# A Fourier layer's loads, spectrum scalings, joins and conditioning rows put in another order

## The chip, the cores and the metric

The kernel runs on one core of one Trainium2 chip. The metric is device time in microseconds (us); the median of three runs of the kernel before is 1674.48 us (1673.05 to 1675.82). The engines are PE (matrix products), DVE (vector), ACT (activations and copies), POOL (a second vector engine) and SP, whose queue issues nearly all loads.

## The reference, cut to what matters

The program is two blocks of a transformer for 256 latent tokens and 256 context tokens of width 1024: a Fourier layer with a gated feed-forward, a differential-attention layer with a feed-forward, then a recurrent layer with 32 experts. The change touches the first layer alone:

```python
sh1, sc1, g1, sh2, sc2, g2 = jnp.split(silu(c)[:, None, :] @ w_ada[0] + b_ada[0], 6, axis=-1)   # and the same for c_ctx
h = rms_norm(x, norm_gain[0, 0]) * (1 + sc1) + sh1
hg = h.astype(jnp.float32).reshape(b, l, FNET_GROUPS, FNET_GROUP_DIM)          # 8 groups of 128 channels
y = jnp.fft.fftn(hg, axes=(1, 3), norm='ortho').real.reshape(b, l, D_MODEL)
x = x + g1 * (y @ w_out + b_out)
x = x + g2 * swiglu(modulate(rms_norm(x, norm_gain[0, 1]), sh2, sc2), ffn_w_in[0], ffn_w_out[0])
```

## The kernel before, in words

Nothing schedules this kernel: each engine runs its instructions in the order in which its function lists them, and waits on named semaphores. All weights come as blocks of 128 x 2048 fp32 (1 MiB) in the order of the list `STREAM`, into a ring of four slots. SP issues block n only when block n-4 is used up, and in order, so that one late release holds all later loads.

Three kinds of blocks matter here. An "ada" block, ("ada", layer, set, k), holds 128 rows of the conditioning weights; PE multiplies it with the conditioning vector in `ada_rows` and adds eight of them up in bank 7, which gives a set of 2048 outputs. `ada_cols` turns such a set into columns (into bank 6), and DVE's `mods` adds the bias. Set 0 of layer 0 holds shift and scale for the first norm, set 1 the gate g1 and the shift of the second norm, set 2 the rest. A "fnet" block holds 256 columns of the layer's output weights; it is split into a high part (`split` on ACT) and a low part (`split` on DVE for three quarters, on POOL for one), and is used up when the low part is made. "fin" blocks, of the feed-forward, follow.

The Fourier layer on 8 groups of channels, c = 0 to 7, goes in these steps:

1. `spectrum(c)`: PE, the transform over tokens, into bank `FIRST[c]`.
2. Scaling: ACT (even c) or DVE (odd c) copies that bank into `Z`, times the norm's gain and scale; then DVE adds the shift to one column pair. Both need the columns of set 0.
3. `channels(c)`: PE, the transform over channels, cosines and sines into bank `SECOND[c]`, which must be free of an earlier spectrum.
4. `keep_sines(c)` (ACT) copies the sines out, `join(c)` (DVE) adds and subtracts them from the cosines into `fsum`, which has two buffers; `high_fnet(c)` (ACT) and the loop at L1704 (POOL) make the high part yh and low part yl. `join(c)` waits for the low part of c-2.
5. Output product c (PE, `mm3`, 24 matmuls), ACT's bias at L1405, DVE's gated addition onto xT at L1927.
6. `sums(1)`, `root`, `normed`: the second norm, and then the feed-forward, which takes all products from L687 on.

In the kernel before, the stream is the eight ada blocks of set 0, fnet 0 and 1, the eight of set 1, fnet 2 and 3, the eight of set 2, then fin 0. The activations xT (2 MiB) are loaded after block 17. The split of fnet 0 stands after the scaling of c = 6 on ACT and DVE and after the fifth low part on POOL; the split of fnet 1 on DVE stands ahead of `mods(1)`.

Of the kernel before, what the change touches and what calls it, by code (L numbers as in the profile page):

```python
# [11 lines left out]
ALU = mybir.AluOpType  # L12
# [72 lines left out]
STREAM = [("ada", 0, 0, k) for k in range(8)]  # L85
_first = BLK["fin", 0, 0]
for _m, _t in enumerate(SPLIT):
    STREAM.append(_t)
    if 1 <= _m - _first <= 24:
        STREAM.append(("ada", 1) + divmod(_m - _first - 1, 8))  # L90
    if _t in (("fnet", 1), ("fnet", 3)):
        STREAM += [("ada", 0, (_t[1] + 1) // 2, k) for k in range(8)]
    for _s, _after in enumerate((("din", DIN[0]), ("fin", 1, 0), ("win", WIN[0]))):
        if _t == _after:
            STREAM += [("ada", 2, _s, k) for k in range(8)]
# [58 lines left out]
def program(nc, wblk, cols_d, cons_d, small_d, wa2_d, xin_d, xnat_d, dft_d, rope_d, out_d):  # L154
    ctx = ExitStack()
    with ctx:
# [349 lines left out]
        FIRST = (0, 1, 2, 3, 4, 5, 0, 1)  # L506
        SECOND = (2, 3, 4, 5, 0, 1, 2, 3)
# [4 lines left out]
        def sines(c):  # L512
            return bank[SECOND[c]][:, 258:512].rearrange("p (s n) -> p s n", s=2)

# [89 lines left out]
        def sync(e):  # L604
# [10 lines left out]
            for n, tag in enumerate(STREAM):  # L615
# [9 lines left out]
                if n == 17:  # L625
# [10 lines left out]
        def pe(e):  # L636
            def ada_rows(n, ks):
                layer, s = SETS[n]
                for k in ks:
# [3 lines left out]
                    if k == 0 and n:  # L643
                        e.wait_ge(*s_arow.at(n - 1))
                    for g in range(4):
# [12 lines left out]
            def ada_cols(n):  # L658
# [3 lines left out]
                for j in range(4):  # L662
                    t = e.matmul(bank[6][:, 8 * j:8 * j + 8], arow[:, j * P:(j + 1) * P], con("sel"), start=True, stop=True)
# [27 lines left out]
            def spectrum(c):  # L691
                if c >= 6:
                    if c % 2:
                        e.wait_ge(*s_zv.at(c - 6))
                    else:
                        e.wait_ge(*s_za.at(c - 6))
# [9 lines left out]
            def channels(c):  # L706
                e.wait_ge(*s_dc.at(c))
                held = c + 2
# [5 lines left out]
                else:  # L714
                    e.wait_ge(*s_d2s.at(c - 6))
# [11 lines left out]
            spectrum(5)  # L727
            ada_rows(0, range(4, 8))
            e.wait_ge(s_cons, 16)
            ada_cols(0)  # L730
            spectrum(6)
            spectrum(7)
            for c in range(KC):
                channels(c)
            MODS = {0: (1, range(3)), 1: (1, range(3, 6)), 2: (1, range(6, 8)), 4: (2, range(2)), 5: (2, range(2, 5)), 6: (2, range(5, 8))}
            for c in range(KC):
                b, m = c // 2, c % 2
                ws = parts(("fnet", b), KC)
                if c == 0:
                    e.wait_ge(*s_d2s.at(2))  # L740
# [9 lines left out]
                if c == 3:  # L750
# [560 lines left out]
        def act(e):  # L1311
# [57 lines left out]
            e.activation(xsq, xsq, ACT.Sqrt, bias=eps, scale=1.0 / D).then_inc(*s_xroot.up(0))  # L1369
            arow_of(0)  # L1370
# [10 lines left out]

            e.wait_ge(*s_a0.at(0))
            for c in range(KC):
                if c % 2 == 0:
                    e.wait_ge(*s_d1.at(c))
                    for s in range(2):
                        t = e.activation(Z[:, c, s, :], bank[FIRST[c]][:, s * L:(s + 1) * L], ACT.Copy, scale=NORM_A[0, s][:, c:c + 1])
                    t.then_inc(*s_za.up(c))
                if c >= 3:
                    keep_sines(c - 3)  # L1390
                if c >= 4:
                    high_fnet(c - 4)
                if c == 6:
                    split(4)
            for c in range(5, KC):
                keep_sines(c)
                high_fnet(c - 1)
            high_fnet(KC - 1)
            for c in range(KC):
# [6 lines left out]
                if c == 2:  # L1406
# [279 lines left out]
        def pool(e):  # L1686
# [16 lines left out]

            for c in range(KC):  # L1704
                e.wait_ge(*s_d2h.at(c))
                e.tensor_tensor(yl[:, c, :], fsum[:, c % 2, :, :].rearrange("p s n -> p (s n)"), yh[:, c, :].bitcast(F32), ALU.subtract).then_inc(*s_d2l.up(c))
                if c == 4:
                    split(1)
# [85 lines left out]
        def dve(e):  # L1794
# [11 lines left out]
            def mods(n):  # L1806
                layer, half = SETS[n]
                e.wait_ge(*s_adat.at(n))
                pv = bank[6][:, 0:32].rearrange("p (j g s) -> p s g j", j=4, g=4)
# [75 lines left out]
            for t in range(4):  # L1885
                e.tensor_scalar(fs[:, t, :], fbase[:, t % 2, :], xrec[:, t:t + 1], None, ALU.mult).then_inc(*s_fs.up(t))
            mods(0)
# [11 lines left out]
            e.wait_ge(*s_a0.at(0))  # L1899
            for c in range(KC):  # L1900
                if c % 2:
                    e.wait_ge(*s_d1.at(c))
                    for s in range(2):
# [692 lines left out]
```

## Time and profile before

| | us |
|---|---|
| median of three runs | 1674.48 |
| the profiled execution's own time | 1671.34 |
| its span in the trace | 1669.5 |
| PE busy | 1497.8 (90%) |
| DVE busy | 776.8 (47%) |
| ACT busy | 488.5 (29%) |
| POOL busy | 212.5 (13%) |
| chain that ended last: PE 72%, DMA 11%, DVE 10%, ACT 4% | |

The profiled execution lies 3.1 us under the median. Its time is 1.8 us more than its span. The page of the profile cuts the span in 40 slices of 42 us, and the whole of the Fourier layer and the second norm is in the first four. In these PE is busy 5, 8, 8 and 7 tenths, against mostly 9 behind them. From slice 30 on the DMA engines move 426 GB/s without a gap: the experts.

### The profile page before, as it was taken

To read this page: it belongs to the slowest core of one execution; us is meant where nothing else is said; L and a number is where in the kernel's file an instruction comes from. 1 tells how busy PE (TensorE), PEld (TensorE's weight loads), DVE (VectorE), ACT (ScalarE), POOL (GpSimd) and SP (SyncE) were. 2 spreads that over 40 slices of the span, in tenths; PEclk is the share of its full clock that TensorE was granted. 3 is DMA by queue.
4 is the path that set the end of the run, shared out by engine and by line. 5 is a ranking of instruction groups with operands and counts; after the bars stand their busy time and mean duration, and the time that the engine had idled before them with its cause. 6 is when DMAs were issued, how large, how long until landed. Compare 5 with 4: busy or idle time off the path is not lost.

```text
span 1669.5 us, 20736 instructions
## 1 busy us (share of the span) xinstructions
PE 1497.8 (90%) x8410; PEld 1074.3 (64%) x8410; DVE 776.8 (47%) x1317; ACT 488.5 (29%) x985; POOL 212.5 (13%) x168
## 2 busy tenths in 40 slices
PE   5887999999999899989999888876899999999896
PEld 3554878877777798777999857765433434334333
DVE  0326766766544987655555557765211011100102
ACT  2314222222344445544444543632101000000001
POOL 0300111111111362001222111320000000000000
PEclk9889999999999999999999998987999999999999
DMA  8474554553324532118454473223599999999992
GB/s 350 176 302 171 197 184 170 201 195 133 139 88 164 213 116 77 51 40 314 177 183 159 140 287 140 103 101 151 245 426 426 427 426 427 427 426 427 426 427 121
DMA packets 54420, 390.46 MB, mean 234 GB/s; under 512 B 6048, under 2 KB 6192, under 8 KB 7728
## 3 DMA queue, kind: packets, MB, share of 16 engines
q1 hardware_dynamic: 53744, 387.72, 58.7%
q8 instruction: 69, 1.13, 0.3%
q10 hardware_dynamic: 576, 1.36, 0.2%
q14 instruction: 31, 0.25, 0.0%
HBM read 388.01 MB, written 1.05 MB: 233 GB/s over the span
## 4 chain that ended last, share of the span: by engine, by line
PE 72%; DMA 11%; DVE 10%; ACT 4%; issue 1%; DVEq 0%; SPq 0%; ACTq 0%; PEldq 0%
PE twin L687 44%; PE twin L1171 15%; DMA ring<-in_wblk 11%; PE twin L1227 3%; DVE wlo L1804 2%; PE twin L674 2%; ACT whi L1323 2%; PE twin L646 2%; PE twin L877 1%; PE twin L1161 1%; PE twin L701 1%; PE twin L901 1%; DVE Hl L1868 1%; DVE rst L1859 1%; DMA xnat<-in_xnat 1%
## 5 line engine op out<-in xcount | busy, mean ns | idle before, releaser
L1804 DVE TENSOR_TENSOR wlo<-ring,whi 128x512 fp32r<-128x512 f32 (+1 forms) x306 | 272.6, 919 | 110.0 <-ACT whi L1323 108.4
L687 PE MATMUL twin<-Hh,whi 128*128 128x256 f32 (+1 forms) x864 | 287.6, 333 | 15.1 <-DVE Hl L1868 8.5
L687 PE MATMUL twin<-Hl,whi 128*128 128x256 f32 (+1 forms) x864 | 284.5, 329 | 0.0
L687 PE MATMUL twin<-Hh,wlo 128*128 128x256 f32 (+1 forms) x864 | 284.3, 329 | 0.0
L1323 ACT ACTIVATE whi<-ring 128x512 fp32r<-128x512 f32 (+1 forms) x408 | 225.0, 612 | 174.6 <-PE twin L687 149.7
L1702 POOL TENSOR_TENSOR wlo<-ring,whi 128x512 fp32r<-128x512 f32 x102 | 151.6, 1486 | 796.6 <-ACT whi L1323 796.6
L1171 PE MATMUL twin<-ring,xg 128*64 128x512 f32 x1024 | 227.7, 598 | 16.9 <-ACT xT L1664 8.2
L687 PEld LDWEIGHTS twin<-Hh,whi 128*128 128x128 f32 x864 | 166.8, 193 | 37.7 <-issue 11.8
L687 PE MATMUL twin<-hsp,whi 128*128 128x512 f32 (+1 forms) x704 | 178.4, 345 | 12.9 <-DVE hsp L1961 9.8
L1171 PEld LDWEIGHTS twin<-ring,xg 128*64 128x64 f32 x1024 | 76.1, 137 | 158.3 <-issue 146.1
L687 PEld LDWEIGHTS twin<-Hh,wlo 128*128 128x128 f32 x864 | 166.7, 193 | 13.9
L687 PEld LDWEIGHTS twin<-Hl,whi 128*128 128x128 f32 x864 | 167.0, 193 | 13.4
L687 PEld LDWEIGHTS twin<-hsp,whi 128*128 128x128 f32 x704 | 124.0, 195 | 30.9 <-issue 11.8
L2392 DVE TENSOR_TENSOR rst<-rst,twin 128x512 f32<-128x512 f32 x16 | 11.0, 688 | 238.4 <-PE twin L1171 213.3
L687 PE MATMUL twin<-hsp,wlo 128*128 128x512 f32 (+1 forms) x352 | 120.4, 342 | 0.0
L1171 PE MATMUL twin<-ring,xT 128*64 128x512 f32 x512 | 113.3, 595 | 0.0
L687 PE MATMUL twin<-whi,Hh 128*128 128x256 f32 x352 | 102.9, 292 | 3.7 <-DVE Hl L1868 2.4
L687 PE MATMUL twin<-wlo,Hh 128*128 128x256 f32 x352 | 99.8, 283 | 0.0
L687 PE MATMUL twin<-whi,Hl 128*128 128x256 f32 x352 | 99.8, 283 | 0.0
L1961 DVE TENSOR_TENSOR hsp<-hid,hsp 128x512 fp32r<-128x512 f32 (+1 forms) x88 | 50.3, 579 | 86.9 <-ACT hsp L1447 85.9
L2397 DVE COPY tmp<-twin 128x512 f32<-128x512 f32 x16 | 11.1, 692 | 155.9 <-PE twin L1171 155.9
L1171 PEld LDWEIGHTS twin<-ring,xT 128*64 128x64 f32 x512 | 35.4, 137 | 69.5 <-issue 69.5
(333 smaller groups left out, 1905.2 us busy)
## 6 DMA issues: line engine op xcount, KB each, us to landing
ring<-in_wblk SPq DMA_DIRECT2D x362, 1024.0 KB, 10.7
xnat<-in_xnat SPq DMA_DIRECT2D x4, 512.0 KB, 6.7
xT<-in_xin SPq DMA_DIRECT2D x1, 2048.0 KB, 12.0
ring<-in_wblk SPq DMA_DIRECT2D x4, 512.0 KB, 3.9
out<-hTm SPq DMA_DIRECT2D x1, 1024.0 KB, 3.8
small<-in_small SPq DMA_DIRECT2D x1, 738.0 KB, 8.5
att<-in_rope ACTq DMA_DIRECT2D x1, 512.0 KB, 5.0
dft<-in_dft ACTq DMA_DIRECT2D x1, 384.0 KB, 6.4
```

What stands on the lines that cost most here:

```text
L646: t = e.matmul(bank[7][32 * g:32 * g + 32, :], cact[:, 1 if layer == 2 else 0, k, :], w[:, g * 512:(g + 1) * 512], start=k == 0, stop=k == 7)
L674: t = e.matmul(out, ones, NORM_SQ[r][:, c, 0:n], start=c == 0, stop=c == KC - 1)
L687: t = e.matmul(out, a, b, start=start and n == 0, stop=stop and n == 2)
L701: t = e.matmul(bank[FIRST[c]][:, s * L:(s + 1) * L], xnat[:, 2 * s + t2, c * P:(c + 1) * P], fs[:, 2 * s + t2, :], start=t2 == 0, stop=t2 ...
L877: t = e.matmul(score_bank(j)[:, c * L2:(c + 1) * L2], qT[pr, h, qt * P:(qt + 1) * P], kT[pr, h, :], start=True, stop=True)
L901: t = e.matmul(bank[7][:, (j % 2) * P:(j % 2 + 1) * P], WT[:, j % 6, k * P:(k + 1) * P], vt[:, h // 2 % 2, k, (h % 2) * P:(h % 2 + 1) * P] ...
L1171: t = e.matmul(out[64 * i:64 * i + 64, :], lhs(kcs + kk, i), ws[i][:, kk, :], start=start and kk == 0, stop=stop and kk == 3)
L1227: t = e.matmul(acc(c), osb[:, p % 2, c * P:(c + 1) * P], Sw[:, p, :], start=p == 0 and c % 2 == 0, stop=p == NP - 1, skip_group_check=True)
L1323: e.activation(hi, w, ACT.Copy).then_inc(*s_hi.up(m, h))
L1702: e.tensor_tensor(lo, w, hi.bitcast(F32), ALU.subtract).then_inc(*s_log.up(m, 1))
L1804: e.tensor_tensor(lo, w, hi.bitcast(F32), ALU.subtract).then_inc(*s_lov.up(m, h))
L1961: e.tensor_tensor(hsp[:, k % nsp, 1, 0:n], hid[:, k, 0:n], hsp[:, k % nsp, 0, 0:n].bitcast(F32), ALU.subtract).then_inc(*s_hpl.up(layer, h ...
```

## The change

Seven things are put in another place. (1) Stream: fnet 0 comes after six blocks of set 0, the last two blocks of set 0 and set 1 follow it, then fnet 1, fnet 2, five blocks of set 2, fnet 3, three blocks of set 2; xT is issued after block 19. (2) The split of fnet 0 stands early: on ACT ahead of the copy of set 0's rows, on DVE behind the scaled token waves, on POOL ahead of its loop. (3) Banks: `spectrum` has seven banks instead of six, so that spectrum 6 moves ahead of the last four rows of set 0 and only spectrum 7 waits for a scaling; `channels(c)` takes the bank that spectrum c+1 has left, instead of that of c+2, and the columns of set 0 go to bank 7. (4) DVE and ACT scale first, and join later. (5) Five of set 1's row blocks stand between the `channels` products, the other three after output product 0; its columns come after product 1 instead of 3. (6) Set 2's rows stand two by two after products 3 to 6. (7) The split of fnet 1 on DVE, until now ahead of `mods(1)`, is now the first thing of the loop behind it, that is behind `mods(1)` and behind the wait for xT.

On PE, at the end of set 0's rows, the order before was this (L701 is `spectrum`, L716 and L717 `channels`, L663 the columns, L646 an ada row block):

```order
L663 MATMUL twin<-cons,arow 128x8 [waits ada_rows,cons_landed]
L663 MATMUL twin<-cons,arow 128x8 x3
L701 MATMUL twin<-fs,xnat 128x256 [waits spectrum_scaled_act]
L701 MATMUL twin<-fs,xnat 128x256 x3
L701 MATMUL twin<-fs,xnat 128x256 [waits spectrum_scaled_dve]
L701 MATMUL twin<-fs,xnat 128x256 x3
L716 MATMUL twin<-Z,dft 128x258 [waits spectrum_scaled_act,spectrum_shifted]
L717 MATMUL twin<-Z,dft 128x254
L716 MATMUL twin<-Z,dft 128x258 [waits spectrum_scaled_dve,spectrum_shifted]
L717 MATMUL twin<-Z,dft 128x254
```

And it is now this (L704 is `spectrum`, L719 and L720 `channels`, L669 the columns, L652 a row block):

```order
L669 MATMUL twin<-cons,arow 128x8 [waits ada_rows,cons_landed]
L669 MATMUL twin<-cons,arow 128x8 x3
L704 MATMUL twin<-fs,xnat 128x256 [waits spectrum_scaled_act]
L704 MATMUL twin<-fs,xnat 128x256 x3
L719 MATMUL twin<-Z,dft 128x258 [waits spectrum_scaled_dve,spectrum_shifted]
L720 MATMUL twin<-Z,dft 128x254
L719 MATMUL twin<-Z,dft 128x258 [waits spectrum_scaled_act,spectrum_shifted]
L720 MATMUL twin<-Z,dft 128x254
L652 MATMUL twin<-ring,cact 32x512 [waits modulation,ada_rows,ring1_landed]
L652 MATMUL twin<-ring,cact 32x512 x3
L719 MATMUL twin<-Z,dft 128x258 [waits spectrum_scaled_dve,spectrum_shifted]
```

One spectrum instead of two stands behind the columns, and a row block of set 1 behind the second channel product. On DVE, behind the last join, the order before was this (L1895 to L1897 are the last join, L1804 the split of fnet 1 and then of fnet 2, L1812 is `mods(1)`, L1927 the addition onto xT):

```order
L1897 TENSOR_TENSOR fsum<-twin,qsum 128x2x127
L1804 TENSOR_TENSOR wlo<-ring,whi 128x512 [waits weights_high] x3
L1812 TENSOR_TENSOR mod<-twin,cols 128x16 [waits ada_columns]
L1812 TENSOR_TENSOR mod<-twin,cols 128x16
L1927 SCALAR_TENSOR_TENSOR xT<-tmp,mod,xT 128x256 [waits fnet_out,x_landed,modulation]
L1927 SCALAR_TENSOR_TENSOR xT<-tmp,mod,xT 128x256
```

And it is now this (L1902 ends the last join, L1816 is `mods(1)`, L1808 the split of fnet 1, L1944 the addition):

```order
L1902 TENSOR_TENSOR fsum<-twin,qsum 128x2x127
L1816 TENSOR_TENSOR mod<-twin,cols 128x16 [waits ada_columns]
L1816 TENSOR_TENSOR mod<-twin,cols 128x16
L1808 TENSOR_TENSOR wlo<-ring,whi 128x512 [waits weights_high,x_landed,modulation]
L1808 TENSOR_TENSOR wlo<-ring,whi 128x512 [waits weights_high] x2
L1944 SCALAR_TENSOR_TENSOR xT<-tmp,mod,xT 128x256 [waits fnet_out]
L1944 SCALAR_TENSOR_TENSOR xT<-tmp,mod,xT 128x256
```

The split of fnet 1, on which output product 2 waits, now waits for `x_landed` itself. The diff:

```diff
@@ -82,14 +82,15 @@
     return BW // 2 if tag[0] == "fout" and tag[3] == 5 else BW
 
 
-STREAM = [("ada", 0, 0, k) for k in range(8)]
+STREAM = [("ada", 0, 0, k) for k in range(6)]
+FRONT = {0: [(0, 6), (0, 7)] + [(1, k) for k in range(8)], 2: [(2, k) for k in range(5)], 3: [(2, k) for k in range(5, 8)]}
 _first = BLK["fin", 0, 0]
 for _m, _t in enumerate(SPLIT):
     STREAM.append(_t)
     if 1 <= _m - _first <= 24:
         STREAM.append(("ada", 1) + divmod(_m - _first - 1, 8))
-    if _t in (("fnet", 1), ("fnet", 3)):
-        STREAM += [("ada", 0, (_t[1] + 1) // 2, k) for k in range(8)]
+    if _t[0] == "fnet":
+        STREAM += [("ada", 0, s, k) for s, k in FRONT.get(_t[1], ())]
     for _s, _after in enumerate((("din", DIN[0]), ("fin", 1, 0), ("win", WIN[0]))):
         if _t == _after:
             STREAM += [("ada", 2, _s, k) for k in range(8)]
@@ -503,14 +504,17 @@
         fbase = dft[:, 256:768].rearrange("p (t n) -> p t n", t=2)
         xsq, xrec = tiny[:, 0:4], tiny[:, 4:8]
         zflat = Z.rearrange("p c s n -> p (c s n)")
-        FIRST = (0, 1, 2, 3, 4, 5, 0, 1)
-        SECOND = (2, 3, 4, 5, 0, 1, 2, 3)
+        FIRST = (0, 1, 2, 3, 4, 5, 6, 0)
+        SECOND = (1, 2, 3, 4, 5, 6, 0, 1)
 
         def cosines(c):
             return bank[SECOND[c]][:, 0:258].rearrange("p (s n) -> p s n", s=2)
 
...
+        def turned_rows(n):
+            return bank[6] if n else bank[7]
 
         def fnet_bank(c):
@@ -622,7 +626,7 @@
                     e.wait_ge(*s_rel.at(*STREAM[n - RING2]))
                 w = width(tag)
                 e.dma_start(block_of(tag)[:, 0:w], wblk[n, :, 0:w]).then_inc(landed(tag)[0], 16)
-                if n == 17:
+                if n == 19:
                     e.dma_start(xT[:, :, :], xin_d).then_inc(s_x, 16)
                 if n == 30:
                     e.dma_start(small[:, :], small_d).then_inc(s_small, 16)
@@ -642,6 +646,8 @@
                     e.wait_ge(*landed(tag))
                     if k == 0 and n:
                         e.wait_ge(*s_arow.at(n - 1))
+                        if n == 1:
+                            e.wait_ge(*s_mod.at(0, 1))
                     for g in range(4):
                         t = e.matmul(bank[7][32 * g:32 * g + 32, :], cact[:, 1 if layer == 2 else 0, k, :], w[:, g * 512:(g + 1) * 512],
                                      start=k == 0, stop=k == 7)
@@ -660,7 +666,7 @@
...
-                    t = e.matmul(bank[6][:, 8 * j:8 * j + 8], arow[:, j * P:(j + 1) * P], con("sel"), start=True, stop=True)
+                    t = e.matmul(turned_rows(n)[:, 8 * j:8 * j + 8], arow[:, j * P:(j + 1) * P], con("sel"), start=True, stop=True)
                 t.then_inc(*s_adat.up(n))
...
@@ -689,11 +695,8 @@
 
 
             def spectrum(c):
-                if c >= 6:
-                    if c % 2:
-                        e.wait_ge(*s_zv.at(c - 6))
-                    else:
-                        e.wait_ge(*s_za.at(c - 6))
+                if c == 7:
+                    e.wait_ge(*s_za.at(0))
                 for s in range(2):
                     for t2 in range(2):
                         if c == 0:
@@ -705,14 +708,14 @@
 
             def channels(c):
                 e.wait_ge(*s_dc.at(c))
-                held = c + 2
+                held = c + 1
                 if held < KC:
                     if held % 2:
                         e.wait_ge(*s_zv.at(held))
                     else:
                         e.wait_ge(*s_za.at(held))
                 else:
-                    e.wait_ge(*s_d2s.at(c - 6))
+                    e.wait_ge(*s_d2s.at(0))
                 e.matmul(cosines(c), cd, Z[:, c, :, 127:256], start=True, stop=True)
                 e.matmul(sines(c), sd, Z[:, c, :, 0:127], start=True, stop=True).then_inc(*s_d2.up(c))
@@ -725,19 +728,21 @@
             ada_rows(0, range(2, 4))
             spectrum(4)
             spectrum(5)
+            spectrum(6)
             ada_rows(0, range(4, 8))
             e.wait_ge(s_cons, 16)
             ada_cols(0)
-            spectrum(6)
             spectrum(7)
+            BETWEEN = {1: (0,), 2: (1,), 4: (2,), 5: (3,), 7: (4,)}
             for c in range(KC):
                 channels(c)
-            MODS = {0: (1, range(3)), 1: (1, range(3, 6)), 2: (1, range(6, 8)), 4: (2, range(2)), 5: (2, range(2, 5)), 6: (2, range(5, 8))}
+                ada_rows(1, BETWEEN.get(c, ()))
+            MODS = {0: (1, range(5, 8)), 3: (2, range(2)), 4: (2, range(2, 4)), 5: (2, range(4, 6)), 6: (2, range(6, 8))}
             for c in range(KC):
                 b, m = c // 2, c % 2
                 ws = parts(("fnet", b), KC)
                 if c == 0:
-                    e.wait_ge(*s_d2s.at(2))
+                    e.wait_ge(*s_d2s.at(3))
                 if c >= 5:
                     e.wait_ge(*s_fna.at(c - 5))
                 for k in range(KC):
@@ -747,7 +752,7 @@
                 t.then_inc(*s_wmm.up("fnet", b, m))
                 if c in MODS:
                     ada_rows(*MODS[c])
-                if c == 3:
+                if c == 1:
                     ada_cols(1)
                 if c == 6:
                     sums(1, range(4))
@@ -1367,6 +1372,7 @@
             e.wait_ge(*s_zero.at("eps"))
             e.wait_ge(*s_xsum.end())
             e.activation(xsq, xsq, ACT.Sqrt, bias=eps, scale=1.0 / D).then_inc(*s_xroot.up(0))
+            split(4)
             arow_of(0)
@@ -1379,22 +1385,21 @@
                 e.wait_ge(*s_d2s.at(c))
                 e.activation(yh[:, c, :], fsum[:, c % 2, :, :].rearrange("p s n -> p (s n)"), ACT.Copy).then_inc(*s_d2h.up(c))
 
+            def scale_spectrum(c):
+                e.wait_ge(*s_d1.at(c))
+                for s in range(2):
+                    t = e.activation(Z[:, c, s, :], bank[FIRST[c]][:, s * L:(s + 1) * L], ACT.Copy, scale=NORM_A[0, s][:, c:c + 1])
+                t.then_inc(*s_za.up(c))
+
             e.wait_ge(*s_a0.at(0))
+            scale_spectrum(0)
+            scale_spectrum(2)
             for c in range(KC):
-                if c % 2 == 0:
-                    e.wait_ge(*s_d1.at(c))
-                    for s in range(2):
-                        t = e.activation(Z[:, c, s, :], bank[FIRST[c]][:, s * L:(s + 1) * L], ACT.Copy, scale=NORM_A[0, s][:, c:c + 1])
-                    t.then_inc(*s_za.up(c))
-                if c >= 3:
-                    keep_sines(c - 3)
-                if c >= 4:
-                    high_fnet(c - 4)
-                if c == 6:
-                    split(4)
-            for c in range(5, KC):
                 keep_sines(c)
-                high_fnet(c - 1)
+                if c < 2:
+                    scale_spectrum(4 + 2 * c)
+                if c:
+                    high_fnet(c - 1)
             high_fnet(KC - 1)
             for c in range(KC):
@@ -1403,7 +1408,7 @@
                 if c >= 4:
                     e.wait_ge(*s_fnx.at(c - 4, 1))
                 e.activation(tmp[:, c % 4, :], fnet_bank(c)[:, :], ACT.Identity, bias=col("fb", c)).then_inc(*s_fna.up(c))
-                if c == 2:
+                if c == 0:
                     arow_of(1)
                 if c == 6:
@@ -1701,11 +1706,10 @@
                     e.wait_ge(*s_hi.at(m, 1))
                     e.tensor_tensor(lo, w, hi.bitcast(F32), ALU.subtract).then_inc(*s_log.up(m, 1))
 
+            split(1)
             for c in range(KC):
                 e.wait_ge(*s_d2h.at(c))
                 e.tensor_tensor(yl[:, c, :], fsum[:, c % 2, :, :].rearrange("p s n -> p (s n)"), yh[:, c, :].bitcast(F32), ALU.subtract).then_inc(*s_d2l.up(c))
-                if c == 4:
-                    split(1)
             split(BLK["din", 0] + 1)
 
 
@@ -1884,6 +1888,7 @@
             e.wait_ge(*own_v.now())
             for t in range(4):
                 e.tensor_scalar(fs[:, t, :], fbase[:, t % 2, :], xrec[:, t:t + 1], None, ALU.mult).then_inc(*s_fs.up(t))
+            split(4)
             mods(0)
             gains(0)
@@ -1896,25 +1901,37 @@
                 e.tensor_tensor(out[:, :, 1:128], p[:, :, 1:128], q, ALU.subtract)
                 e.tensor_tensor(out[:, :, 129:256], p[:, :, 1:128][:, :, ::-1], q[:, :, ::-1], ALU.add).then_inc(*s_d2s.up(c))
 
-            e.wait_ge(*s_a0.at(0))
-            for c in range(KC):
+            def scale_spectrum(c):
+                e.wait_ge(*s_d1.at(c))
+                for s in range(2):
+                    t = e.tensor_scalar(Z[:, c, s, :], bank[FIRST[c]][:, s * L:(s + 1) * L], NORM_A[0, s][:, c:c + 1], None, ALU.mult)
+                t.then_inc(*s_zv.up(c))
+
+            def shift_spectrum(c):
                 if c % 2:
-                    e.wait_ge(*s_d1.at(c))
-                    for s in range(2):
-                        t = e.tensor_scalar(Z[:, c, s, :], bank[FIRST[c]][:, s * L:(s + 1) * L], NORM_A[0, s][:, c:c + 1], None, ALU.mult)
-                    t.then_inc(*s_zv.up(c))
                     e.wait_ge(*s_zv.at(c))
                 else:
                     e.wait_ge(*s_za.at(c))
                 shift = mod[:, 0, :].rearrange("p (s x) -> p s x", s=2)[:, :, c:c + 1]
                 e.scalar_tensor_tensor(Z[:, c, :, 127:128], shift, math.sqrt(2.0), Z[:, c, :, 127:128], ALU.mult, ALU.add).then_inc(*s_dc.up(c))
-                if c >= 3:
-                    join(c - 3)
-                if c == 6:
-                    split(4)
-            for c in range(5, KC):
+
+            e.wait_ge(*s_a0.at(0))
+            scale_spectrum(1)
+            shift_spectrum(0)
+            scale_spectrum(3)
+            shift_spectrum(1)
+            shift_spectrum(2)
+            scale_spectrum(5)
+            shift_spectrum(3)
+            join(0)
+            scale_spectrum(7)
+            shift_spectrum(4)
+            shift_spectrum(5)
+            join(1)
+            shift_spectrum(6)
+            shift_spectrum(7)
+            for c in range(2, KC):
                 join(c)
-            split(8)
             mods(1)
             e.wait_ge(*s_mod.at(1, 1))
             e.wait_ge(s_x, 16)
```

## Rows read from the trace of the kernel before

**Rows 1.** The chain that ended last, 0 to 200 us (start, length, what).
```profile
27.09 7.86 DMA ring<-in_wblk
...
45.89 0.43 PE twin L716 x2
...
58.07 0.86 PE twin L716 x2
...
61.67 5.96 PE twin L687 x24
...
78.27 13.66 DMA ring<-in_wblk
...
101.91 7.90 PE twin L687 x24
...
111.67 5.71 PE twin L687 x24
117.37 2.71 PE twin L646 x24
...
128.48 3.63 PE twin L674 x8
...
137.64 0.69 ACT tmp L1405
...
142.63 0.70 ACT rst L1345
```

**Rows 2.** Stretches: us, busy (x count) by engine, granted clock, DMA share, GB/s.
```profile
47.00:61.00 14.00, 8.80 (x27) 6.08 (x25) 10.59 (x32) 8.89 (x21) 7.00 (x6) 0.80 0.00 0
...
52.00:56.00 4.00, 0.06 (x1) 0.01 (x1) 3.78 (x8) 2.86 (x6) 2.33 (x2) 0.92 0.00 0
56.00:62.00 6.00, 5.78 (x13) 4.22 (x14) 2.60 (x10) 2.29 (x6) 3.13 (x4) 0.50 0.00 0
...
77.50:89.50 12.00, 10.60 (x62) 6.13 (x55) 0.00 (x0) 0.00 (x0) 0.00 (x0) 1.00 1.01 427
...
101.90:106.40 4.50, 4.49 (x11) 3.52 (x12) 4.04 (x8) 0.00 (x0) 0.00 (x0) 0.50 0.65 233
```

**Rows 3.** Single issues on SP's queue: start, length (blocks 8, 11 and 12, xT).
```profile
31.74 0.33 SPq L624 DMA_DIRECT2D ring<-in_wblk  x1
...
36.12 0.33 SPq L624 DMA_DIRECT2D ring<-in_wblk  x1
...
61.66 0.33 SPq L624 DMA_DIRECT2D ring<-in_wblk  x1
...
77.46 0.43 SPq L626 DMA_DIRECT2D xT<-in_xin  x1
```

**Rows 4.** Loads up to 170 us: xT's issue to landing; least, median, most of 35 blocks.
```profile
xT<-in_xin SPq DMA_DIRECT2D x1, 2048.0 KB, 12.0
...
DMA to landing us min/median/max: 4.7/7.8/16.0
```

**Rows 5.** Timeline around set 0's rows: start, length, [idle before and its releaser].
```profile
26.96 3.72 PE L701 MATMUL twin<-fs,xnat 128*128 128x256 f32 x16
...
34.99 1.06 PE L646 MATMUL twin<-ring,cact 128*32 128x512 f32 x8 [1.60 <-DMA ring<-in_wblk]
```

**Rows 6.** Timeline of POOL's last three low parts.
```profile
61.53 2.55 POOL L1706 TENSOR_TENSOR yl<-fsum,yh 128x512 fp32r<-128x512 f32 x2
64.49 1.29 POOL L1706 TENSOR_TENSOR yl<-fsum,yh 128x512 fp32r<-128x512 f32 x1 [0.40 <-ACT yh L1380]
```

**Rows 7.** Timeline around output products 2 and 4.
```profile
64.96 3.67 DVE L1804 TENSOR_TENSOR wlo<-ring,whi 128x512 fp32r<-128x512 f32 x3 [1.22 <-ACT whi L1323]
...
80.61 0.50 PE L687 MATMUL twin<-yh,whi 128*128 128x512 f32 x1
...
99.97 1.89 DVE L1804 TENSOR_TENSOR wlo<-ring,whi 128x512 fp32r<-128x512 f32 x3
...
101.91 0.79 PE L687 MATMUL twin<-yh,whi 128*128 128x512 f32 x1 [5.60 <-DVE wlo L1804]
```

More of the change, by code:

```diff
@@ L1808, in mods @@
                 e.wait_ge(*s_adat.at(n))
-                pv = bank[6][:, 0:32].rearrange("p (j g s) -> p s g j", j=4, g=4)
+                pv = turned_rows(n)[:, 0:32].rearrange("p (j g s) -> p s g j", j=4, g=4)
                 for s in range(1 if layer == 2 else 2):
```

## The prediction, made before the changed kernel had run

> **What bounds the kernel now.** I read the page's slices first: PE is short of work in the first 160 us and at 9 tenths in most of the rest, so a change to the Fourier layer is judged there. Then the chain of waits over that stretch [rows 1]. From 27 to 46 us it goes through the load of set 0's last ada block; from 46 to 61.7 through the channel products and what ACT and DVE do for them; again from 69 us (the row for 78.27 to 91.93 is the longest) through loads; then through the split of fnet 2, and from 101.9 us through PE alone, up to the copy behind output product 7 at 137.64 and the second norm's root at 142.63. Third, why the loads are late, since the engines can move 427 GB/s [rows 2]: from 47 to 61 us they move nothing. The issues on SP's queue say why [rows 3]: block 11 goes at 36.12 and block 12 only at 61.66, because it waits for fnet 0's low part, which POOL makes behind the low parts yl of five channel groups. Those 25 us without an issue cost the waits for loads behind 69 us and, as xT (2 MiB) and fnet 2 are queued together, the wait ahead of product 4: PE idle 5.60 us until 101.91 [rows 7]. The clock adds to it: PE all but idles from 52 to 56 us and is then granted 0.50 of full speed, that is 1.2 GHz, for 6 us, and again in product 4 [rows 2].
>
> The chain stays in this layer's steps up to the norm, and from the root on nothing is changed. So what product 7 gains, the kernel gains.
>
> **Set 0's rows: later by 3.9 us.** Spectrum 6 now stands ahead of rows 4 to 7. Sixteen spectrum matmuls take 3.72 us [rows 5], so eight take 1.8. Set 0's last block is now block 8, which waits for the use of row 4, as block 8 does now, at 31.74 [rows 3]: 31.7 + 1.8 and a hand-over, 33.6 us. A block takes 4.7 us at least from issue to landing, 7.8 in the median [rows 4]: landed at 38.3 to 41.4. It is alone but for a block issued a microsecond later, so I take 38.9, against 34.99 before [rows 5]. The early split of fnet 0 costs nothing: ACT, DVE and POOL have nothing else between 14 and 36 us; its block is the seventh and lands ahead of row 6's (an estimate: at 32 us), and the split is done by 36, ahead of the rows.
>
> **Behind the columns: earlier by 3.3 us.** One spectrum is left instead of two; the pair took 6.57 us at half clock, from 39.31 to the first channel product at 45.89 [rows 1]. PE idles here as before, so I keep the half clock: 3.3 us. Channel product 0 starts at 45.9 + 3.9 - 3.3 = 46.5.
>
> **Channel products: 13.2 us instead of 15.8.** Before, 45.9 to 61.7. One takes 0.87 us at full clock and 1.7 at half (the first part alone 0.43 and 0.86 [rows 1]); an ada row block 0.90 (2.71 for three). With DVE and ACT free of the split, the hole from 52 to 56 us goes. Two products at half clock, 3.4; six at full, 5.2; five row blocks, 4.6 with their switches: 13.2, so output product 0 starts at 59.7. From below, all at full clock, 11.6; from above, everything as slow as before with the rows added, 15.8 + 4.6 = 20.4. I take 13.2, since the rows fill the time in which DVE scales and shifts. Next late is POOL: its low parts take 1.28 us each, join c waits for low part c-2, and the last three started 2.96 us apart, first to third [rows 6]: 1.5 us each from a first low part at about 52 to 53 ends the eighth at 63 to 64.5; product 0, with 0.7 us for each of its eight steps, asks for it at 64.7. It just holds; where it doesn't, product 0 ends later by the difference. Product 0 takes 5.96 [rows 1] and ends at 65.7, against 67.6.
>
> **xT and fnet 1: product 2 starts at 81.4, 0.8 us later than now.** SP sends fnet 2 when row 5 of set 1 is used, 1 us behind product 0, at 66.7; then an ada block, xT at 68.0 and another ada block. The queue is empty by then. xT has 4 MiB up to its own end: at 427 GB/s [rows 2] 9.8 us, and 2.2 of the least 4.7 are no data, so 78.7; by its own row, 12.0 us from issue [rows 4], 80.0. I take 79.4. DVE's split of fnet 1 now stands behind this wait, though its block has landed by 65 us. It takes 1.89 us, or 3.67 beside other work [rows 7]; nothing runs beside it, so 1.9 and a hand-over: 81.4. PE has done product 1 and the columns at 75.3 and idles 6 us. Queued behind the same wait on DVE are the additions onto xT and the split of fnet 2; they take some 5 us and product 4 asks for that split only at 94.
>
> The Trainium skill ("DMA: Bandwidth & Descriptors", "Queues, rings and completion order") says that each ring's descriptors are taken in order, though completions need not be. By that xT would not share with the ada block issued behind it, and the sum would be 0.7 us less. The row of xT is the other end, since xT took 12.0 us with blocks issued ahead of it and behind it; no row here shows which shared.
>
> **From product 2 to product 7: 47.6 us instead of 57.0.** Before, 80.61 to 137.64 [rows 1, 7]. Now: one product at half clock for its first 4.5 us, since PE has idled, 7.90 as product 4 took; five at 5.7, 28.5; eight rows of set 2 at 0.90, 7.2; four sums, 3.6 [rows 1]: 47.2. What goes is the wait ahead of product 4, two rows of set 1 and its columns. Fnet 3 is issued at about 93.6 and asked for at 109; set 2's last block at about 109.6 and asked for 8 us later, at the median of 7.8, so 0.4 us for that. Product 7 ends at 129.0, against 137.6.
>
> **Sum.** -8.6 us. Against the profiled execution's own time 1671.3 - 8.6 = 1662.7. That execution lies 3.1 under the median, so against the median of the runs: 1674.5 - 8.6 = 1665.9, which I call 1666. The parts on the path: rows +3.9, spectrum -3.3, channels -2.6 (product 0 is earlier by 1.9 to 2.0), +2.7 between products 0 and 2 through the wait for xT, and -9.4 behind it; their rounding makes 0.1.
>
> **Rivals.**
> - *xT is no wait to speak of* (18 in 100). Channels at full clock throughout (-1.6), xT taken in order (-0.7), the clock not falling ahead of product 2 (-2.2): -13.1, and 1661. For it: rows between the products keep PE busier. Against it: in the trace PE idles four microseconds and the clock falls each time, and nothing shortens the 2 MiB.
> - *The channel products are as slow as now, and rows come on top* (8 in 100): 20.4 instead of 13.2, +7.2, so -1.4 and 1673, no change that can be measured. For it: POOL's low parts and the two buffers of the joins are as before, and the new scalings stand ahead of the joins. Against it: the hole in the trace is the split's, and it is gone.
> - *The gain is given back later* (4 in 100): the feed-forward would then wait for its weights. Against it: from fin 0 on the order of loads is the old one, and its blocks are issued ten microseconds ahead of the norm's end. 1674.
> - *Slower, by xT alone* (4 in 100). DVE holds the split of fnet 1 until xT lands, so from product 2 on each microsecond of xT is one of the kernel. It turns the sum where xT lands later than 79.4 + 8.6 = 88.0 us. With set 0's last block at the median (+2.5), the slow channels (+7.2) and the 16.0 us that the slowest block took [rows 4] in place of 12.0 (+4.0) it would land at 93, and the kernel take 1679.5. Against it: it needs all three.
> - *The forecast* (66 in 100), within 3.5 us either way.
>
> **Numbers.** A measurement of this kernel tells about 0.2%, 3.3 us, from no change. Faster by more: the forecast, its faster rival and a little of the middle, 0.86; within: 0.10; slower by more: 0.04. The range: the fast rival's 13.1 and something for luck in the landings give 1660 below; the bounds of the channel term (20.4 at the top, of which I leave out the last third) and of set 0's last block give 1671 above.
>
> **What would show it.** Right: no stretch without loads between 36 and 58 us but a short one; set 0's last row waits for its load until 38 or 39 us; the hole at 52 to 56 is gone; product 0 starts near 60; PE idles from 75 to 81 us and the first split of fnet 1 on DVE starts when xT lands; no wait ahead of product 4; the norm's root near 134. Wrong: product 0 starting behind 64 us; xT landing behind 83; a load wait in set 2's rows of over 2 us; or a feed-forward from the root on that is longer than the 1528.7 us which the trace has between the root at 142.63 and the end of the profiled execution's time.

## The result, and the profile after

The changed kernel takes 1662.79 us in the median of 7 runs (1661.20 to 1667.64), against 1673.05 for the kernel before (7 runs): a ratio of 0.9937, 95% interval 0.9921 to 0.9953, or 8 to 13 us. The forecast was 1666, with 8.6 us to gain. In the profiled executions (1671.34 and 1664.10 us of their own) the norm's root starts 7.15 us earlier, and what lies from there to the end of the span is equal: 1526.9 and 1526.8 us.

Not all of the difference ahead of the root is the change's. Both kernels begin with the same sixteen spectrum matmuls (spectra 0 and 1, behind the same waits), and in the two traces these took:

```profile
14.19 5.48 PE twin L701 x16
...
14.06 6.50 PE twin L704 x16
```

The first line is the kernel before, the second the changed one; in the traces of the nine runs below they took 5.41 to 6.42 us. Why is not known. They end at 19.67 and 20.57 us, and counted from there the root comes 8.05 us earlier.

The chain of waits of the changed kernel (start, length, what; it answers to [rows 1]):

```profile
34.36 4.79 DMA ring<-in_wblk
...
41.06 1.86 PE twin L669 x8
...
44.33 3.78 PE twin L704 x8
48.11 0.86 PE twin L719 x2
...
61.03 0.99 PE twin L652 x8
62.02 5.69 PE twin L693 x24
67.71 1.90 PE twin L652 x16
...
70.00 7.21 DMA xT<-in_xin
77.20 4.33 issue
81.53 1.91 DVE wlo L1808 x3
...
83.48 13.31 PE twin L693 x48
...
130.49 0.69 ACT tmp L1410
...
135.48 0.70 ACT rst L1350
```

Between 48 and 68 us the chain is now PE alone. The only load behind it is xT, and then comes what hung on it: the split of fnet 1 at 81.53 and output products 2 and 3 at 83.48, 13.31 us for the two. Behind them nothing but PE up to 130.49. The same in stretches (us, busy by engine, granted clock, DMA share, GB/s; the first answers to [rows 2]):

```profile
47.00:61.00 14.00, 14.00 (x71) 7.78 (x72) 6.27 (x26) 7.24 (x17) 6.33 (x5) 0.88 0.63 243
...
72.00:80.00 8.00, 4.90 (x27) 4.08 (x25) 0.26 (x2) 2.83 (x6) 1.26 (x1) 1.00 1.03 439
83.00:90.00 7.00, 6.52 (x19) 5.20 (x20) 4.50 (x9) 0.00 (x0) 0.00 (x0) 0.64 0.59 201
```

PE is busy for all of 47 to 61 us, where it had been for 8.80 of 14, and the loads move 243 GB/s there instead of 0. PE is idle for 3.1 of the 8 us up to 80 and is granted 0.64 behind that. The timeline of PE at the two waits that are left (start, length, and in brackets the idle time before with its releaser; they answer to [rows 5, 7]):

```profile
39.19 1.07 PE L652 MATMUL twin<-ring,cact 128*32 128x512 f32 x8 [2.62 <-DMA ring<-in_wblk]
...
83.48 0.80 PE L693 MATMUL twin<-yh,whi 128*128 128x512 f32 x1 [6.58 <-DVE wlo L1808]
```

And the issues on SP's queue, against [rows 3], with xT's time from issue to landing, against [rows 4]:

```profile
40.32 0.33 SPq L628 DMA_DIRECT2D ring<-in_wblk  x1
52.13 0.33 SPq L628 DMA_DIRECT2D ring<-in_wblk  x1
...
70.00 0.43 SPq L630 DMA_DIRECT2D xT<-in_xin  x1
...
xT<-in_xin SPq DMA_DIRECT2D x1, 2048.0 KB, 11.5
```

The stretch without an issue has shrunk from 25.5 us to 11.8, and xT goes out 7.5 us earlier.

### The profile page after: what moved, and what is told of

Same layout as the page of the kernel before. It is cut to its first block, busy times and chain, and to the rows that moved or that the text cites. A ratio compares the mean times of both kernels' runs of the same rounds, so it can differ in the third digit from the quotient of the medians.

```text
span 1662.3 us, 20736 instructions
## 1 busy us (share of the span) xinstructions
PE 1497.0 (90%) x8410; PEld 1075.2 (65%) x8410; DVE 773.9 (47%) x1317; ACT 489.2 (29%) x985; POOL 211.9 (13%) x168
## 4 chain that ended last, share of the span: by engine, by line
PE 75%; DVE 9%; DMA 9%; ACT 4%; issue 1%; SPq 0%; DVEq 0%; ACTq 0%; PEldq 0%
PE twin L693 45%; PE twin L1176 15%; DMA ring<-in_wblk 9%; PE twin L1232 4%; DVE wlo L1808 2%; PE twin L680 2%; PE twin L652 2%; ACT whi L1328 1%; PE twin L704 1%; PE twin L1166 1%; PE twin L882 1%; PE twin L906 1%; DVE Hl L1872 1%; DVE rst L1863 1%; DMA xnat<-in_xnat 0%
## 5 line engine op out<-in xcount | busy, mean ns | idle before, releaser
L1808 DVE TENSOR_TENSOR wlo<-ring,whi 128x512 fp32r<-128x512 f32 (+1 forms) x306 | 271.6, 915 | 133.2 <-ACT whi L1328 127.4
L693 PE MATMUL twin<-hsp,whi 128*128 128x512 f32 (+1 forms) x704 | 174.9, 340 | 12.9 <-DVE hsp L1978 9.8
L693 PEld LDWEIGHTS twin<-hsp,whi 128*128 128x128 f32 x704 | 121.1, 191 | 30.7 <-issue 11.8
```

Source lines behind the costliest of these rows:

```text
L693: t = e.matmul(out, a, b, start=start and n == 0, stop=stop and n == 2)
L1808: e.tensor_tensor(lo, w, hi.bitcast(F32), ALU.subtract).then_inc(*s_lov.up(m, h))
```

## The experiments

Each profile tells when output products 0 and 2 and the root start, of one execution. Whole times of one kernel spread over 4 to 11 us. These points spread less, but they do spread: product 0 starts at 62.02 in the changed kernel and at 60.97 in run 1, whose edit stands behind it. Nearly all of that is the first sixteen spectrum matmuls, which no edit touches: from their end (E in the table) to product 0 the changed kernel and runs 1 to 3 take 41.36 to 41.46 us. So the table has the root's distance from E too. Ratios are to the kernel before, run beside each kernel.

| | E | product 0 | product 2 | root | root less E | median | ratio [interval] |
|---|---|---|---|---|---|---|---|
| before | 19.67 | 61.67 | 80.61 | 142.63 | 122.96 | 1673.05 | |
| changed | 20.57 | 62.02 | 83.48 | 135.48 | 114.91 | 1662.79 | 0.9937 [0.9921, 0.9953] |
| 1: fnet 1's split back | 19.61 | 60.97 | 75.83 | 125.54 | 105.93 | 1653.73 | 0.9892 [0.9872, 0.9912] |
| 2: xT early | 20.67 | 62.13 | 80.33 | 131.76 | 111.09 | 1661.62 | 0.9934 [0.9919, 0.9948] |
| 3: old scaling order | 20.50 | 61.93 | 83.14 | 135.21 | 114.71 | 1666.88 | 0.9954 [0.9936, 0.9973] |
| 4: set 0 first | 19.87 | 57.15 | 78.12 | 130.36 | 110.49 | 1661.46 | 0.9929 [0.9911, 0.9947] |
| 5: 1 and 4 | 20.42 | 57.65 | 72.50 | 122.22 | 101.80 | 1654.51 | 0.9877 [0.9855, 0.9899] |
| 6: no rows between | 20.10 | 56.16 | 92.91 | 144.70 | 124.60 | 1675.30 | 1.0006 [0.9991, 1.0021] |
| 7: 6 and a late split | 19.70 | 66.17 | 102.80 | 154.42 | 134.72 | 1685.54 | 1.0076 [1.0054, 1.0098] |
| 8: before, early split | 20.05 | 57.75 | 76.78 | 139.38 | 119.33 | 1672.09 | 0.9995 [0.9982, 1.0008] |
| 9: 5 and xT early | 20.04 | 57.97 | 73.36 | 123.07 | 103.03 | 1655.18 | 0.9896 [0.9871, 0.9921] |

**1. The split of fnet 1 ahead of mods(1) again.**

```diff
             for c in range(2, KC):
                 join(c)
+            split(8)
             mods(1)
```

> The changed kernel with one edit: DVE's split of fnet 1 stands ahead of mods(1) again, as in the kernel before, and no longer waits for xT. Theory A (the wait for xT in front of product 2 comes only from where this split stands): product 2 starts right behind the columns of set 1, at 76.9 us instead of 83.5, and at full clock (products 2 and 3 in 11.4 us instead of 13.3); product 7 ends near 122.0 instead of 130.5; the kernel takes 8.5 us less than the changed one, near 1654.3. Rival B (the loads are the bound, and the wait only moves): a wait of 4 us or more for fnet 2, fnet 3 or set 2's blocks shows up behind product 2, product 7 ends at 126 or later, and the kernel gains 4 us or less, 1659 or more.

```profile
69.35 5.69 PE twin L693 x24
75.04 0.79 PE twin L669 x8
75.83 11.03 PE twin L693 x48
...
125.54 0.70 ACT rst L1350
```

In the chain product 2 follows right behind the columns, products 2 and 3 take 11.03 us instead of 13.31, and the root comes 9.9 us earlier, 9.0 counted from E. Theory A holds, and the ratio, 0.9892, shows it in the whole time: its interval lies clear of the changed kernel's. One line's place had cost more than the whole change gained (9.0 against 8.05 us, both from E).

**2. xT behind block 12.**

```diff
-                if n == 19:
+                if n == 12:
```

> The changed kernel with one edit: xT is issued behind block 12, at about 40 us, where the queue has room, instead of behind block 19. DVE's split of fnet 1 stays where the change put it. Theory A: xT lands near 50 us, DVE's split then waits only for mods(1) at 77.1 us, and product 2 starts at 79.1 instead of 83.5, with PE idle for 2 us, too short for its clock to fall; the kernel takes 6.3 us less than the changed one, near 1656.5. Rival B (2 MiB put in early make the blocks behind them late): set 1's rows 0 to 3 wait for loads between the channel products, product 0 starts 2 us or more later than 62.0, and the kernel gains 4 us or less.

```profile
76.19 0.80 PE twin L669 x8
...
77.31 2.98 DVE wlo L1808 x3
...
80.33 12.75 PE twin L693 x48
...
131.76 0.70 ACT rst L1350
```

```profile
80.33 0.50 PE L693 MATMUL twin<-yh,whi 128*128 128x512 f32 x1 [3.35 <-DVE wlo L1808]
```

No row waits and product 0 is no later, so rival B's mechanism falls, though its number, 4 us or less, is met. Theory A's price is missed: the gain is 3.7 us at the root, not 6.3. The split behind mods(1) takes 2.98 us instead of 1.91, beside ACT's and POOL's split of fnet 2 (that these slow it is argued, not tried), so PE idles 3.35 us instead of the 2 forecast, and its clock fell (12.75 for two products). Its whole time can't be told apart from the changed kernel's. An early xT takes away a part of the wait; another place for the split takes away all of it.

**3. The old order of scalings and joins** (on ACT the loop is scaling c, sines c-3, high part c-4).

```diff
-            scale_spectrum(1)
-            shift_spectrum(0)
...
-            for c in range(2, KC):
-                join(c)
+            for c in range(KC):
+                if c % 2:
+                    scale_spectrum(c)
+                shift_spectrum(c)
+                if c >= 3:
+                    join(c - 3)
+            for c in range(5, KC):
+                join(c)
```

> The changed kernel with the old order of scalings and joins on DVE and ACT: scaling c, shift c, join c-3, in one loop (on ACT scaling c, sines c-3, high part c-4). Everything else as in the changed kernel. Theory A (the ada rows between the channel products and POOL's low parts set the pace, so the scalings need not be first): product 0 starts within 1 us of 62.0 and the kernel is within 1 us of the changed one. Rival B (scalings first is what lets the channel products run): the later channel products wait for scalings, product 0 starts 3 us or more later, and the kernel takes 3 us or more over the changed one.

```profile
61.93 5.67 PE twin L693 x24
...
135.21 0.70 ACT rst L1350
```

Products and root are where the changed kernel has them, to 0.3 us: scaling first gives nothing at the root (0.2 us, counted from E). The median is 4 us higher, but the intervals of the ratios overlap, and the difference lies behind the root (last section).

**4. Fnet 0 behind all of set 0, split in ACT's and DVE's idle time.**

```diff
-STREAM = [("ada", 0, 0, k) for k in range(6)]
-FRONT = {0: [(0, 6), (0, 7)] + [(1, k) for k in range(8)], 2: ...
+STREAM = [("ada", 0, 0, k) for k in range(8)]
+FRONT = {0: [(1, k) for k in range(8)], 2: ...
...
-            split(4)
             arow_of(0)
...
             scale_spectrum(0)
             scale_spectrum(2)
+            split(4)
...
-            split(4)
             mods(0)
...
             shift_spectrum(3)
+            split(4)
             join(0)
```

> The changed kernel with fnet 0 behind all eight blocks of set 0, and its split on ACT and DVE in the time in which both idle while PE does spectrum 7 and the first channel product (on ACT behind scaling 2, on DVE behind shift 3). Theory A (fnet 0 ahead of set 0's last two blocks costs the load wait at 36 to 39 us, and nothing else hangs on it): set 0's last row waits for no load and ends at 37.5 instead of 40.3, product 0 starts 3 us earlier, near 59, and the kernel takes 3 us less than the changed one, near 1660. Rival B (the split in the middle holds up scalings and joins): product 0 starts at 61 or later and the kernel gains 1 us or less.

```profile
32.60 3.62 PE twin L652 x32
...
36.24 0.61 ACT arow L1334
...
57.15 5.69 PE twin L693 x24
...
78.12 13.55 PE twin L693 x48
...
130.36 0.70 ACT rst L1350
```

The four last rows of set 0 now run without a load wait and end at 36.2; product 0 starts 4.9 us earlier and the root 5.1; counted from E, 4.2 and 4.4. That is still more than theory A's 3. The four rows take 3.6 us instead of 7.0, and the columns behind them 1.04 instead of 1.86, as in the kernel before; the spectrum takes 3.78 us as it did.

**5. Both.** The edits of runs 1 and 4.

> Both of the edits that moved the norm's root (the point at which the Fourier layer is done): the split of fnet 1 ahead of mods(1), and fnet 0 behind set 0 with its split in the idle time. Theory A (the two waits are independent): the root's start falls by the sum of the two, from 135.5 to 120.7 us, product 2 starts at 71 and the kernel takes some 15 us less than the changed one, near 1648. Rival B (the loads become the bound once both waits are gone): a load wait of 3 us or more for fnet 1, fnet 2 or an ada block appears, and the root comes at 123.5 or later.

```profile
57.65 5.66 PE twin L693 x24
...
72.50 11.03 PE twin L693 x48
...
122.22 0.70 ACT rst L1350
```

The root falls by 13.3 us where the sum of the two is 15.1, with no load in the chain behind the rows of set 0, so rival B falls. Theory A's mechanism holds and its figure does not: product 2 comes 1.5 us later than forecast. The forecast had added up two shifts that each held some luck of the first spectra. Counted from E the shifts are 9.0 and 4.4 us, and both together give 13.1, 0.3 less than their sum; from product 0 to the root it is 64.57 us here and in run 1 alike. This is the kernel with the earliest root; in the whole time it is not told apart from run 1.

**6. No rows between the channel products.**

```diff
-            BETWEEN = {1: (0,), 2: (1,), 4: (2,), 5: (3,), 7: (4,)}
+            BETWEEN = {}
...
-            MODS = {0: (1, range(5, 8)), ...
+            MODS = {0: (1, range(8)), ...
```

> The changed kernel without set 1's rows between the channel products: all eight stand behind output product 0. Theory A (the rows between keep the ring moving): product 0 starts near 57 instead of 62.0, but blocks 13 to 17 are issued only behind it, rows 4 to 7 wait for loads until 76 us, xT lands near 86 and product 2 starts near 88.5; the root comes 5 us later than in the changed kernel, near 140.5. Rival B (the ring has room enough): product 2 starts at 84 or earlier, and the root is within 1 us of the changed kernel's 135.5.

```profile
67.65 8.04 DMA ring<-in_wblk
...
78.10 8.81 DMA xT<-in_xin
...
92.91 13.11 PE twin L693 x48
...
144.70 0.70 ACT rst L1350
```

```profile
40.59 0.33 SPq L628 DMA_DIRECT2D ring<-in_wblk  x1
...
65.93 0.33 SPq L628 DMA_DIRECT2D ring<-in_wblk  x1
```

The old hole of 25 us in the issues is back, although fnet 0 is used up by 36 us; the load wait behind it and a late xT (issued at 78.10) follow. Product 0 starts at 56.16 but then takes 8.7 us, since POOL's low parts pace it. The root is 9.2 us later than in the changed kernel, and even 2.1 later than in the kernel before (9.7 and 1.6 from E). Theory A had the mechanism; its 5 us were too few, and product 2, forecast at 88.5, came at 92.91.

**7. The same, with fnet 0's split behind the joins.**

```diff
-            split(4)
             mods(0)
...
             for c in range(2, KC):
                 join(c)
+            split(4)
             mods(1)
```

(and likewise behind the high parts on ACT and the low parts on POOL)

> The changed kernel without rows between the channel products, as in the run above, and with the split of fnet 0 behind the high parts on ACT, behind the joins on DVE and behind the low parts on POOL. Theory A (the early release of one slot is what the gain hangs on, since SP issues in order): no block is issued from 41 to about 63 us, product 0 starts near 64, xT lands near 94, product 2 starts near 96 and the root comes at 148 or so, later than in the kernel before (142.6). Rival B (the gain is in the order of PE's and DVE's work): the root stays within 2 us of the run above.

```profile
66.17 8.65 PE twin L693 x24
...
102.80 12.93 PE twin L693 x48
```

Behind run 6 the root loses another 9.7 us: 10.0 of them are product 0, which waits for the split itself (66.17 against 56.16). So here the early split pays through its own place on DVE, and not, as theory A put it, through a freed slot: xT is issued 9.9 us later than in run 6, no more than product 0. Theory A's direction holds, but product 2 comes 7 us and the root 6 us later than it forecast.

**8. The kernel before with the early split alone.**

```diff
-STREAM = [("ada", 0, 0, k) for k in range(8)]
+STREAM = [("ada", 0, 0, k) for k in range(6)]
...
+    if _t == ("fnet", 0):
+        STREAM += [("ada", 0, 0, k) for k in (6, 7)]
...
+            split(4)
             mods(0)
...
-                if c == 6:
-                    split(4)
```

(and likewise on ACT and POOL)

> The kernel before with one part of the change alone: fnet 0 behind six blocks of set 0, and its split early on ACT, DVE and POOL; the rest of the stream, the banks, the scalings, the rows and the place of fnet 1's split as before. Theory A (the early split alone frees only three more blocks, since block 13 then waits for fnet 1's split behind the joins): the hole of the channel products goes, product 0 starts near 60, xT is issued within 2 us of its old 77.5, and the root comes near 140.5, 2 us earlier than in the kernel before. Rival B (the early split is the whole of the gain): the root comes near 135.5 and the kernel takes 7 to 10 us less than the kernel before.

```profile
39.46 0.33 SPq L626 DMA_DIRECT2D ring<-in_wblk  x1
...
65.76 1.28 SPq L626 DMA_DIRECT2D ring<-in_wblk  x3
```

```profile
55.27 0.67 PE L718 MATMUL twin<-Z,dft 128*128 128x258 f32 x2 [1.23 <-DVE Z L1905]
```

The split alone brings 3.3 us at the root (3.6 from E), less than can be told in the whole time. PE's hole in the channel products shrinks from 3.96 to 1.23 us, which is the early split's own gain: product 0 starts 3.9 us earlier. But the hole in the issues is as long as before, 26 us: fnet 1 is block 9 here, so block 13 waits for its split, which stands behind the joins and ends just ahead of 65.76. Rival B falls; xT went out at 73.71, 3.7 us earlier, which theory A had put at 2 at most.

**9. Run 5 with xT behind block 12.** The edits of runs 1, 2 and 4.

> The fastest kernel so far (fnet 1's split ahead of mods(1), fnet 0 behind set 0), with xT also issued behind block 12. Theory A (no product waits for xT any more, so its place is free): product 2 starts at 72.5 and the root at 122.2, both within 0.5 us of the kernel without this edit, and the times can't be told apart from its 1654.5. Rival B (xT still holds back something, such as fnet 2's split behind the additions onto it): the root comes 1 us or more earlier.

```profile
54.48 11.29 DMA ring<-in_wblk
...
65.81 1.06 PE twin L652 x8
...
73.36 11.03 PE twin L693 x48
...
123.07 0.70 ACT rst L1350
```

With no product waiting for xT, its early place gives nothing, and the last row of set 1 now waits 0.2 us for a load that took 11.29. Product 2 and the root are 0.86 and 0.85 us later than in run 5, outside theory A's 0.5, on the losing side; 0.32 of it lies ahead of product 0. Rival B, a root 1 us earlier, falls.

## Why the prediction was right

- **Set 0's rows:** forecast to start their last at 38.9 us, 39.19 by the trace. The mechanism, block 8 behind row 4, is the 4.79 us load in the chain; run 4 takes it away. That the number is met to 0.3 us is luck: block 8 went at 34.36 instead of 33.6, as the first spectra took longer, and landed 4.79 us later instead of 5.3. Counted from E the rows come 3.3 us later than before, not 3.9.
- **Behind the columns:** forecast 3.3 us earlier, 46.5 for channel product 0; it started at 48.11. This is the term that was mis-sized. The columns took 1.86 us instead of 1.04: PE had idled 2.62 us ahead of the last row instead of 1.60, and from 41 to 43 us it was granted 0.50 where the columns before had 1.00; without that wait (run 4) they take 1.04. And one spectrum took 3.78 us, not half of 6.57. It takes 3.78 in run 4 as well, and the kernel before was granted 0.50 from 39.3 to 43.1 us and 0.65 behind that: the pair's first half had been the dear one. Together 1.3 us, so -2.0 instead of -3.3.
- **Channel products:** 13.9 us by the trace, 13.2 forecast. DVE's and ACT's hole is gone as said; the 0.7 us more are the switches between rows and products (a row takes 0.99 us, and a product behind one 1.06 instead of 0.87), less 0.4 us by which the full clock came back sooner. That scaling first would fill time was no term, and run 3 shows it is worth nothing at the root. POOL's pace just holds, as forecast; run 6 shows the limit once the rows are taken away.
- **The wait for xT:** product 2 at 83.48, forecast 81.4, and the 2.1 us between them are there at product 0 already (62.02 for 59.7). From fnet 2's issue at 68.77 to the split at 81.53 are 12.8 us, forecast 12.7. The Trainium skill ("DMA: Bandwidth & Descriptors", "Queues, rings and completion order") has each ring's descriptors taken in order; by that the prediction's estimate was 12.0, with xT sharing nothing with the block behind it. The measured 12.8 stands, and no run here tells which blocks shared.
- **From product 2 to product 7:** 47.0 us by the trace, 47.6 forecast, with the half clock in product 2.
- **The sum:** 7.15 us at the root against 8.6, or 8.05 counted from E, and 8 to 13 in the whole time. Term by term, from E: +3.3, -2.0, -1.9, +2.5 and -10.0, against +3.9, -3.3, -2.6, +2.7 and -9.4. The misses partly cancel, so that the sum is better than its terms. The rivals: xT was a wait to speak of (run 1); the channel products were not slow; nothing was given back behind the root (1526.8 us against 1526.9); xT landed at 81.5, far from the 88.0 at which it would have turned the sum.

What the prediction didn't name is what lets the ring move. It laid the hole in the issues to fnet 0's late split alone. Runs 6 and 8 show that the early split is not enough: without the rows between the channel products the changed kernel is as slow as the kernel before, and with the early split alone the ring stands still for 26 us as it did. Three parts work together; this is read from the order of the stream. Fnet 1 now comes behind set 1, so that rows, which PE can use up at once, fill the slots; the rows between the products use them; and the second of these rows, block 10, can go out only when fnet 0, block 6, is used up, so that this order asks for the early split. With the rows between the products and a late split of fnet 0 the engines would wait for each other, so that it was not run; and the new banks and the places of set 2's rows were not tried alone.

Across the ten kernels the ratio follows the root: the interval of each, times 1673 us, holds the shift of its root but for the changed kernel's (7.15 against 7.9 to 13.2) and run 8's (3.3 against 3.0 at the most). Counted from E the changed kernel's 8.05 is inside and run 8's 3.6 still is not. So the root's figure is the safer one for what this layer gave, and what the whole time shows beyond it (10.3 us between the medians) is not explained.

## What to carry to other kernels

Where one queue issues loads in order into few slots, ask of every slot which instruction gives it back, and put a user of each of the next blocks into any stretch of compute that is longer than a load; one early release only uncovers the next one that is late. When a wait is moved in an engine's order, look at what stands behind it: here a 1.9 us split queued behind a 2 MiB load cost 9 us at the root, more than the 8 that the whole change gained there. Compare such changes by a point in the trace behind which nothing differs, as well as by whole times, and count it from a point ahead of which nothing differs: here that took 1 us of chance out of single traces.

## What the runs showed of the hardware

PE's clock fell after 3.35 us of idle time (run 2, products 2 and 3 in 12.75 us, granted 0.88 from 83 to 90 us) and did not where product 2 followed at once (run 1, 11.03 and 1.00). And whole times of one kernel spread by as much as most edits here are worth: run 3 had its root at the changed kernel's place and its span 6.6 us longer, with 0.956 of full clock granted on the mean against 0.962. Stretches behind the root, of the changed kernel and of run 3:

```profile
850.00:950.00 100.00, 93.72 (x767) 92.15 (x766) 57.71 (x98) 50.22 (x107) 20.19 (x16) 1.00 0.44 159
```

```profile
850.00:950.00 100.00, 94.06 (x750) 92.70 (x749) 56.19 (x93) 47.87 (x103) 19.99 (x16) 0.97 0.44 159
```

The granted clock is 1.00 in the one and 0.97 in the other, in code that is the same. Why it falls in one execution and not in another stays open.
